# A two-block fp32 network on one core: a ring of eight panels split in place, a convolution's taps in two steps, a norm moved back, and other panel rates beside two scans

## The reference, cut to what matters

```python
def _ssd_branch(z, xbc, dt_raw, conv_w, conv_b, dt_bias, a_log, d_skip, norm_g):
    xbc = jax.nn.silu(_dwconv(xbc, conv_w, conv_b))      # 5 taps over the tokens, 1536 channels
    ...
    y_f = _ssd_scan(xs, dt[:, :, 0], A[0], bm, cm)       # 16 heads, forward and backward
    y_b = _flip(_ssd_scan(_flip(xs), _flip(dt[:, :, 1]), A[1], _flip(bm), _flip(cm)))
    ...
    return _group_rmsnorm(y * jax.nn.silu(z), norm_g, SSD_G)

def _mlstm_branch(q, k, v, ig_raw, fg_raw, o_raw, i_bias, f_bias, norm_g):
    ...                                                  # 8 heads of 128, forward and backward
    hn = _head_layernorm((h_f + h_b).reshape(n_b, n_s, ML_W), norm_g, ML_H)
    return (hn * jax.nn.sigmoid(o_raw.astype(F32))).astype(q.dtype)

def second_block(x, p, ...):
    for l in range(DEPTH):
        u = _rmsnorm(h, norm_mix_g[l])
        (s_z, s_xbc, s_dt, g_q, g_f, g_i, g_g, m_q, m_k, m_v, m_i, m_f, m_o,
         gates) = _split(u @ w_in[l], IN_SIZES_2)
        y_ssd, y_hg, y_ml = ...
        h = h + merged @ w_out[l]                        # merged: the gated sum of the three
        ...
```

## Time and profile before

| | us |
|---|---|
| three runs | 2459.04, 2462.45, 2462.49 |
| median | 2462.45 |
| the profiled execution's own time | 2461.96 |
| its span, first to last instruction | 2460.2 |
| PE busy in the span | 2419.2 (98%) |
| VectorE, ScalarE busy | 1779.1 (72%), 1467.6 (60%) |

### The profile page before, as it was taken

One profiled execution on the slowest core, in us unless ns is written; L12 is line 12 of the kernel. 1 busy time (PEld: TensorE's weight loads), 2 busy tenths in 40 slices (PEclk: granted clock), 3 DMA queues, 4 the chain that ended last, 5 costly groups with the idle time before them and its releaser, 6 DMA issues.

```text
span 2460.2 us, 43187 instructions
## 1 busy us (share of the span) xinstructions
PE 2419.2 (98%) x17768; PEld 2219.3 (90%) x17768; DVE 1779.1 (72%) x2840; ACT 1467.6 (60%) x2188; POOL 287.3 (12%) x222
## 2 busy tenths in 40 slices
PE   8999999999999999999999999999999999999998
PEld 8888999988889899799999799998899998899997
DVE  5568675565586755679878887885699778887875
ACT  5547555455476455477655655664678656556654
POOL 0000002000000000001223720000012207500000
PEclk9999999999999999999999999999999999999999
DMA  7554476655544565565567745666555667646663
GB/s 256 157 145 123 153 253 195 200 182 169 141 121 147 179 198 188 172 176 139 138 210 187 196 145 186 188 192 196 161 160 140 177 180 200 181 152 188 190 210 132
DMA packets 358921, 430.51 MB, mean 175 GB/s; under 512 B 20617, under 2 KB 286311, under 8 KB 358469
## 3 DMA queue, kind: packets, MB, share of 16 engines
q1 hardware_dynamic: 341312, 401.72, 53.7%
q10 hardware_dynamic: 14340, 14.93, 3.0%
q0 software_dynamic: 3072, 11.10, 1.5%
HBM read 424.44 MB, written 3.24 MB: 174 GB/s over the span
## 4 chain that ended last, share of the span: by engine, by line
PE 86%; DVE 9%; ACT 3%; issue 1%; DMA 1%; ACTq 0%; POOL 0%; POOLq 0%; DVEq 0%
PE ps L112 84%; DVE wlo L121 2%; PE ps L115 2%; DVE hgQ L121 1%; ACT L118 1%; DVE hgA L148 1%; ACT lnv L118 0%; ACT whi L118 0%; DVE hgkf L121 0%; DMA kT<-in_diff_lambda 0%; DVE hgkb L121 0%; DVE sx L130 0%; DVE sbc L130 0%; DVE hgT L121 0%; ACT sqf L118 0%
## 5 line engine op out<-in xcount | busy, mean ns | idle before, releaser
L121 DVE TENSOR_TENSOR wlo<-wring,whi 128x1024 fp32r<-128x1024 f32 (+1 forms) x768 | 919.8, 1217 | 231.8 <-ACT whi L118 231.2
L118 ACT ACTIVATE whi<-wring 128x1024 fp32r<-128x1024 f32 (+1 forms) x768 | 803.8, 1054 | 411.7 <-PE ps L112 391.9
L112 PE MATMUL ps<-uT,whi 128*128 128x256 f32 x4640 | 814.1, 280 | 5.9 <-DVE wlo L121 5.9
L112 PEld LDWEIGHTS ps<-uT,whi 128*128 128x128 f32 x4640 | 703.1, 188 | 14.9 <-DVE wlo L121 8.5
L112 PE MATMUL ps<-uT,wlo 128*128 128x256 f32 x2320 | 644.4, 278 | 0.0
L112 PEld LDWEIGHTS ps<-uT,wlo 128*128 128x128 f32 x2320 | 436.5, 188 | 0.0
L112 PE MATMUL ps<-xT,whi 128*128 128x256 f32 x2112 | 376.3, 282 | 2.9 <-DVE xT L121 1.7
L112 PEld LDWEIGHTS ps<-xT,whi 128*128 128x128 f32 x2112 | 321.3, 188 | 9.5 <-issue 5.6
L112 PE MATMUL ps<-xT,wlo 128*128 128x256 f32 x1056 | 294.1, 279 | 0.0
L112 PE MATMUL ps<-whi,hid 128*128 128x512 f32 x864 | 270.0, 391 | 0.0
L112 PEld LDWEIGHTS ps<-xT,wlo 128*128 128x128 f32 x1056 | 198.0, 188 | 0.1
(11 more groups left out here) (390 smaller groups left out, 3570.4 us busy)
## 6 DMA issues: line engine op xcount, KB each, us to landing
wring<-in_w_in SPq DMA_DIRECT2D x346, 512.0 KB, 4.3
wring<-in_mlp_w SPq DMA_DIRECT2D x128, 512.0 KB, 4.5
wring<-in_w_up SPq DMA_DIRECT2D x88, 512.0 KB, 4.5
wring<-in_w_down SPq DMA_DIRECT2D x44, 512.0 KB, 4.4
wring<-in_w_branch SPq DMA_DIRECT2D x32, 512.0 KB, 3.4
wring<-in_w_out SPq DMA_DIRECT2D x32, 512.0 KB, 4.5
wring<-in_mem_w_kv SPq DMA_DIRECT2D x16, 512.0 KB, 6.4
wring<-in_w_br_hg SPq DMA_DIRECT2D x16, 512.0 KB, 5.4
```

The lines of the kernel that those rows point to most:

```text
L112: return self.e.matmul(*p, **k) if self.e else Nothing()
L118: return self.e.activation(*p, **k) if self.e else Nothing()
L121: return self.e.tensor_tensor(*p, **k) if self.e else Nothing()
```

## The change

Four things change together.

- The ring: 8 slots of 1088 floats (`WS`), and `wlo` is now the same memory as `wring`, so `split_lo` writes over its own input. A slot is free for the next DMA when TensorE is done with the panel 8 back. `whi` keeps 4 slots, of 1088 floats.
- The panel's place in its slot: 16 floats in for `projB`; for `projA`, `x.off % 64` floats in. With the new bases (slots start at 64 by 256 and are 17 x 256 bytes long, and the arena starts at 64 by 256), a `projB` panel starts at 128 as before, and a `projA` panel starts at the same remainder by 256 as the `x` it is multiplied with: 64 for `xT`, `uT`, `memT`, the hidden pieces of the MLP, `merged` of the second block; 128 for the three named above.
- The taps: VectorE's `ssd_conv` does two taps, and a new step `ssd_taps` the other two after at least one more panel; the bank and the silu wait for the second.
- The norm and the rates: in group 1 VectorE takes t = 0 again (4 instructions) and ScalarE t = 1; one of two idle yields before that norm is gone. The rates are 0.9 for 1.0 and 1.0 for 1.1.

```diff
-NW, WN, NS, LEAD = 5, 1024, 4, 3
+NW, WN, NS, LEAD, WS = 8, 1024, 4, 3, 1088
...
-    K.wring = sb("wring", NW * WN)
-    K.whi, K.wlo = sb("whi", NS * WN, F32R), sb("wlo", NS * WN, F32R)
+    o = (nc.sbuf_base + 31) // 32 * 32
+    K.wring = sb("wring", 48 + NW * WS)[:, 48:48 + NW * WS]
+    K.wlo = nc.alloc_sbuf_tensor_at("wlo", [128, NW * WS], F32R, offset=o + 192)[:, :]
+    K.whi = sb("whi", NS * WS + 16, F32R)
...
-    base = (nc.sbuf_base + 63) // 128 * 128 + 64
+    base = (nc.sbuf_base + 191) // 256 * 256 + 64
...
-        w, s = (i % NW) * WN, (i % NS) * WN
-        p = Panel(i, K.wring[:, w:w + n], K.whi[:, s:s + n], K.wlo[:, s:s + n], nk, nb, parts)
+        at = 16 if rows is None else rows.off % 64
+        w, s = (i % NW) * WS + at, (i % NS) * WS + at
+        p = Panel(i, K.wring[:, w:w + n], K.whi[:, s:s + n], K.wlo[:, w:w + n], nk, nb, parts)
...
-            e.wait_ge(*at(("lo", p.i - NW)))
+            e.wait_ge(*at(("panel", p.i - NW, 1)))
...
+            def late_taps():
+                do("ssd_taps", c, C, *C.late[1:])
+                C.late = None
+            def xbc_proj():
+                for _ in projB(w, SXBC, 1536, uT, out_x):
+                    if C.late and len(panels) > C.late[0]:
+                        late_taps()
+                    yield
+                if C.late:
+                    late_taps()
...
-            yield
             yield
             do("ml_norm", M, c, 1)
...
-        weave((ssd_scan(), 1), (ml_proj(), 1.0))
+        weave((ssd_scan(), 1), (ml_proj(), 0.9))
...
-        weave((ml_scan(), 1), (rest(), 1.1))
+        weave((ml_scan(), 1), (rest(), 1.0))
...
-        for t in range(1 - g, 2):
-            for h in range(4):
-                v = M.H3[:, t, (4 * g + h) * 128:(4 * g + h) * 128 + 128]
-                o = e.activation(v, v, ACT.Identity, bias=nm[:, t, h:h + 1], scale=rs[:, t, h:h + 1])
+        for h in range(4):
+            v = M.H3[:, 1, (4 * g + h) * 128:(4 * g + h) * 128 + 128]
+            o = e.activation(v, v, ACT.Identity, bias=nm[:, 1, h:h + 1], scale=rs[:, 1, h:h + 1])
...
-        for n, i in enumerate((0, 1, 3, 4)):
+        for n, i in list(enumerate((0, 1, 3, 4)))[first:first + 2]:
```

More of the change, by code:

```diff
@@ L428, in do, with panel @@
         steps.append((kind, args))
-    def panel(parts, nk, nb):
+    def panel(parts, nk, nb, rows=None):
         i = len(panels)
         n = nk * nb
-        w, s = (i % NW) * WN, (i % NS) * WN
-        p = Panel(i, K.wring[:, w:w + n], K.whi[:, s:s + n], K.wlo[:, s:s + n], nk, nb, parts)
+        at = 16 if rows is None else rows.off % 64
+        w, s = (i % NW) * WS + at, (i % NS) * WS + at
+        p = Panel(i, K.wring[:, w:w + n], K.whi[:, s:s + n], K.wlo[:, w:w + n], nk, nb, parts)
         panels.append(p)
@@ L449, in projA @@
                 nk = min(step, chunks - k0)
-                p = panel([(0, w[r0 + k0 * 128:r0 + (k0 + nk) * 128, c0 + b0:c0 + b0 + nb])], nk, nb)
+                p = panel([(0, w[r0 + k0 * 128:r0 + (k0 + nk) * 128, c0 + b0:c0 + b0 + nb])], nk, nb, x)
                 do("tokens", p, x, us, k0_ + k0, first and k0 == 0, fin and k0 + nk == chunks)
@@ L468, in rows_first @@
         for j in range(4):
-            p = panel([(0, w[r0 + j * 256:r0 + j * 256 + 256, c0:c0 + 512])], 2, 512)
+            p = panel([(0, w[r0 + j * 256:r0 + j * 256 + 256, c0:c0 + 512])], 2, 512, x)
             by_hand.add(p.i)
@@ L1221, in ssd_proj @@
         def ssd_proj():
-            C.wait = None
+            C.wait = C.late = None
+            def late_taps():
[8 more added lines that the diff above has]
+                    late_taps()
             def out_x(k, m, u):
@@ L1228, in out_x @@
                 do("ssd_conv", c, C, k, u)
+                C.late = (len(panels), k, u)
             def z_proj():
@@ L1231, in z_proj @@
                 yield from projB(w, SZ, 1024, uT, features_to(C.z, ACT.Silu))
-            yield from woven((projB(w, SXBC, 1536, uT, out_x), 1), (z_proj(), 0.67))
+            yield from woven((xbc_proj(), 1), (z_proj(), 0.67))
             do("ssd_silu", C, C.wait)
@@ L2846, in ssd_conv, with ssd_taps, taps @@
         e.wait_ge(*at((C.name, "mid", k)))
-        for n, i in enumerate((0, 1, 3, 4)):
+        taps(c, C, k, u, 0)
+    def ssd_taps(c, C, k, u):
+        taps(c, C, k, u, 2)
+    def taps(c, C, k, u, first):
+        for n, i in list(enumerate((0, 1, 3, 4)))[first:first + 2]:
             f = i - 2
@@ L2961, in ml_norm @@
         e.wait_ge(*now(chain))
[L2962 to L2967, removed]
+        for h in range(4):
+            v = M.H3[:, 0, (4 * g + h) * 128:(4 * g + h) * 128 + 128]
+            o = e.tensor_scalar(v, v, rs[:, 0, h:h + 1], nm[:, 0, h:h + 1], ALU.mult, ALU.add)
+        o.then_inc(*up(chain))
+        e.wait_ge(*now(chain))
         v = slice(512 * g, 512 * g + 512)
         for t in range(2):
-            if t or g:
-                e.wait_ge(*at(("mlhalf", c.l, g, t)))
+            if t:
+                e.wait_ge(*at(("mlhalf", c.l, g)))
             e.wait_ge(*at((M.o.name, t, g)))
@@ L3038, in final_gain @@
         e.tensor_tensor(f.hg.tok(512)[:, t, :], f.h[:, t, 0:512], f.gain.ap[:, 0:512], ALU.mult).then_inc(*up("dve_rows", ("fgain", t)))
-    parts = dict(square_piece=square_piece, split_half=split_half, split_squares=split_squares, split_lo=split_lo, positions=positions, rope_tables=rope_tables, lower_bounds=lower_bounds, split_bank=split_bank, split_bank_scaled=split_bank_scaled,
+    parts = dict(ssd_taps=ssd_taps, square_piece=square_piece, split_half=split_half, split_squares=split_squares, split_lo=split_lo, positions=positions, rope_tables=rope_tables, lower_bounds=lower_bounds, split_bank=split_bank, split_bank_scaled=split_bank_scaled,
                  latent_out=latent_out, latent_norm=latent_norm, kpe_out=kpe_out, mla_rope=mla_rope, scores=scores, weights=weights,
```

2 lines of the change are left out of this document (1 added, 1 removed).

## The result

The changed kernel took **2478.62 us** (median of three: 2473.34, 2478.62, 2479.00) against 2462.45 before: slower by 16 us by the medians; the ratio is 1.0055 (95% interval 1.0042 to 1.0069), 13.5 us. Run again beside other kernels it gave 1.0064 (1.0046 to 1.0082). The forecast was 2453.3, range 2447 to 2463.

What follows compares the result with a forecast made beforehand. TensorE, busy for 2419.2 of 2460.2 us, was taken to bound the kernel. Addresses -5.1, taps -0.4, scan 0, mLSTM's end -0.9 and -1.5, clock -0.8 sum to -8.7: 2461.96 to 2453.3 us, range 2447 to 2463.

Steps and rivals of the forecast that it cites:

- The SSD scan at 0.9: Fewer panels beside the SSD scan's heads: 0 a layer, bounds -1.29 and -1.69 us, and +1.2 us.
- Rival (C): Both scans get slower, 0.22 us a head, as fewer panels fill TensorE's time: 2467.5 us, chance 0.10.
- The clock: Half-clock stretch behind the wait at the mLSTM's end may stay away: -0.8 us, bounds -1.6 and +1.6.
- The addresses: 512-column matmuls with operands starting alike save 2.6 ns each, less those beside the scans: -5.1 us.
- rival (B): Equal starting addresses of panel and operand give nothing: 2458.4 us, chance 0.18.
- The term that I put at 0: `projB` panels stay at 128 with `x` at 64, so their matmuls change by 0.
- The mLSTM's end: Waits on low splits there shrink, with about 0.2 and 0.9 us on `uT`: -0.9 and -1.5 us by layer.
- The taps: Splitting the SSD convolution's taps shortens TensorE's waits on low splits: -0.4 us, bounds -0.7 and +0.5.
- the ring: Low split in place and eight panel slots: 0; panels still land in time, 10.9 us against 4.3.
- Rival (D): A quarter of some 10,000 256-wide matmuls change pace: 11 us either way, 2464 or 2442, chance 0.22, half up.
- the three waits named at the start: TensorE's waits of 8.8 us on low splits, 6.9 on an early DMA, 3.2 on `sE`: larger part of 41 us.

Runs made afterwards that it cites:

- b_rate1: Kernel before with only the SSD scan's rate at 0.9 (mLSTM's stays at 1.1): 2472.46 us, 1.0038 to the kernel before.
- a_fill: Changed kernel with panels beside the SSD scan at 1.0 for the first 12 steps, then 0.9: 2473.57 us, 1.0038 to the kernel before.
- fill_noalign: Changed kernel with every panel at 128 and the SSD scan at 1.0 for 12 steps, then 0.9: 2465.24 us, 1.0006 to the kernel before.
- h_align: Changed kernel with both rates as before and panels at 128, except those multiplied with the first block's `hid`, at 64: 2468.33 us, 1.0023 to the kernel before.
- a_rates_back: Changed kernel with both rates as before (1.0 and 1.1): 2463.65 us, 0.9997 to the kernel before.
- a_rates_noalign: Changed kernel with both rates as before and every panel at 128: 2462.89 us, 0.9999 to the kernel before.
- after_again: Changed kernel run again without an edit: 2479.69 us, 1.0064 to the kernel before.
- a_noalign: Changed kernel with every panel at 128, the rest as changed: 2475.07 us, 1.0041 to the kernel before.
- b_rates: Kernel before with only the two rates of the change (0.9 and 1.0): 2475.55 us, 1.0047 to the kernel before.
- a_rate1_back: Changed kernel with only the SSD scan's rate back at 1.0 (mLSTM's stays at 1.0): 2465.57 us, 1.0016 to the kernel before.
- n_taps_back: Changed kernel with both rates as before, every panel at 128 and all four taps in one step: 2462.81 us, measured once.

## Why the prediction was wrong

**The SSD scan at 0.9, forecast 0: the step that failed.** The working followed VectorE to the scan's end, where a wait stood, and found rightly that the order there changes little; the wait went from 1.29 and 1.69 to 0.20 and 0.29. It never followed the first heads, since PE had no wait there; what could have been seen is VectorE's 0.63 us of idle time on `mxb<-spread`, a transfer that was already late for VectorE and hidden from PE by the panels alone. Its upper bound of +1.2 us a layer, one more split, does stand in front of the weights, but it is the smaller part. Measured: +9.4 us (b_rate1), of which 5.8 are the waits of 2.63 and 3.17; the rest is not placed. The forecast gave a slower kernel 0.14 in all.

**Rival (C)** had the sign, and named the rate; its 2467.5 was the nearest figure and still 11 us short. Its mechanism was another: 0.22 us at each of 48 heads. a_fill and fill_noalign keep 0.9 for all heads behind the twelfth step and take half of the loss and all of it away, so it is not that. VectorE after is busy for 8.80 of 10 us in the stretch of the earlier trace rows: with fewer panels beside it, it had slack, and PE did not wait in mid-scan.

```profile
1355.00:1365.00 10.00, 10.00 (x84) 8.70 (x83) 8.80 (x15) 5.02 (x8) 9.65 (x5) 1.00 0.88 235
```

**The clock, forecast -0.8.** The ledger has +11.9, and the timed runs some 5 on average. I allowed for a drop behind one wait that was there; new waits bring their own. In the first profile each of the waits of 3.8 and 3.6 us costs its length and up to 3.4 us more, (1 - 0.66) x 10, and each of the two of 2.11 us on `uT` 1.7 more. That is not a price to count on: of the ten waits of 2.6 to 4.1 us in the table, the clock fell behind six, by 1.7 or 3.4 us, and stayed at 1.00 behind four, among them 3.24 us in a second execution of the changed kernel. Some drops have no part in it: the one at 50 to 58 us, 1.7 us, is in the profile after and in most others, not in before.

**The addresses, forecast -5.1.** The first half was right: 512-wide matmuls at equal remainders are faster, also at 64 and 64, by 3.5 us in the ledger (rival (B) fell). The gain is a third smaller than forecast, since not all of these matmuls gained 2.6 ns: h_align has 2.0 in `hid`. The term that I put at 0, `projB`, was the error: its own remainders did not change, yet its pace behind a `hid` product did. Net, equal remainders cost 0 (a_rates_back against a_rates_noalign) to 6 us (after_again against a_noalign), which timing does not separate. The Trainium skill, "SBUF — State Buffer", section "SBUF: two separate sides", says that PE never waits on anyone. The forecast took from this that an operand's address costs nothing, which the section itself does not say: it is about engines that contend for a port. h_align, 152 to 147 matmuls by an address alone, disagrees with that reading, though expecting nothing came nearer in time than my -5.1.

**The mLSTM's end, forecast -2.4.** The long waits on low splits went (4.84 us) and two of 2.11 us on `uT` came. I had put those at 0.2 and 0.9 by adding up VectorE's queue with PE arriving as before; at rate 1.0 PE comes to the product sooner, and the split of `uT` behind head 7 starts at 1468.48, after 2.9 us of that head's rows:

```profile
1465.63 0.16 DVE L130 SCALAR_TENSOR_TENSOR sx<-sx 128x4 f32<-128x4 f32 x1
...
1468.48 1.26 DVE L121 TENSOR_TENSOR uT<-ys,uT 128x512 fp32r<-128x512 f32 x2
```

The norm itself is a small gain (0.7 us of waits), and the rate is a loss of 2 (b_rates less b_rate1) to 5 us (a_rate1_back less a_rates_back, by the ratios), intervals overlapping.

**The taps (-0.4) and the ring (0)** were right within what could be timed; the taps' waits are 0.7 us (n_taps_back). The split in place takes 1215 ns for 1217, and panels land in 3.7 us for 4.3. What the working on the ring left out is the other transfers: the row transfer takes 0.4 to 0.7 us longer with it (a_rates_back against before), which costs nothing at the rate 1.0 and lengthens the waits at 0.9. After:

```profile
L121 DVE TENSOR_TENSOR wlo<-wring,whi 128x1024 fp32r<-128x1024 f32 (+1 forms) x768 | 919.5, 1215 | 232.6 <-ACT whi L118 232.0
...
wring<-in_w_in SPq DMA_DIRECT2D x346, 512.0 KB, 3.7
```

**Rival (D)**, the pace: +6.0 us in the profile after, where I had 11 at a chance of 0.11 upwards. It is no rival but a part of every comparison here, and partly caused by the change.

**One reading** was off: the three waits named at the start are 18.9 of the 41 us in which PE is not busy, not the larger part; all waits that the view lists are 32.7.

Open: what sets the pace of a 256-wide stretch, beyond that it is held until something disturbs PE and that a `hid` product at 64 and 64 sets it slow. Whether the equal remainder does that or the panel's start at 64 by itself was not separated; the second block's `hid`, equal at 128 and 128, is not followed by a slow stretch. That the clock falls behind some waits of 2 to 3.4 us and not behind others is also open.

## What to carry to other kernels

When fewer pieces of other work are put between the steps of a pipeline, follow the first steps and the transfers that they issue, not only the waits that the old profile shows: the pieces are also the cover of a transfer, and slack is what the old profile doesn't list. Where TensorE is 98% busy, price a new wait at its length and, as the upper bound, the slow clock that may follow it (0 to 3.4 us here), and look at the pace of the matmuls behind an edit as well as at those in it. And before a gain of 5 us is believed here, the count of matmuls in a window that nobody touched should be the same in both profiles.

## What the runs showed of the hardware

- Matmuls of 256 columns with the same operands at the same addresses, clock 1.00, DMA share 0.58 to 0.66, run at one of two paces, 355 or 342 in 40 us (113 and 117 ns); a stretch of a thousand keeps its pace, and the next execution of the same kernel may have the other.
- The address of the panels of one product alone switches it for the stretch behind: 152 to 147 in 17 us (a_rates_noalign, h_align).
- 512 columns: 174 for 172 in 39 us with stationary and moving operand at the same remainder by 256, at 64 (h_align) as at 128 (`w_down` before), for 64 and 128.
- After PE stood still for 3.8 us its granted clock was 0.66 over 10 us, 2 of them idle. Behind waits of 2.63 and 3.17 us (b_rate1) and 3.24 us (after_again) it stayed at 1.00; behind waits of 2.11 us it fell (0.73 over 1470 to 1475 us, after).
- A transfer of 256 KB that writes two rows to all 128 partitions, issued from ScalarE's queue beside the panel stream, takes 5.5 to 6.3 us until VectorE can use it with five panel slots and 6.2 to 7.0 with eight.
